# Decode-token mixing and slot assignment moved into the tile loop of the output projection

## Chip, cores and metric

The kernel runs on 1 core of one Trainium2 chip. The metric is the device time of one execution in microseconds (us).

## What is computed

One inference step of a one-layer decoder, all in float32, for a prompt of 2048 tokens and for 8 decode samples of one token each ("the sample"). Cut to what matters here:

```python
h  = rmsnorm(x, norm_mix_g); z = h @ w_in                  # 1024 -> 3584 columns
hg = hgrn2_recurrence(...)                                 # 4 heads, state 128 x 128
att = merge_dilations(three windows (128,1), (512,4), (2048,16))   # 8 heads of 64
x  = x + concat(rmsnorm(hg) * silu(zg), att) @ w_out       # 1024 -> 1024
h2 = rmsnorm(x, norm_ffn_g)
group, experts, gates = hier_route(h2, w_rg, w_re)         # 1 of 8 groups, 2 of its 8 experts
x  = x + sum_k gates[k] * (silu(h2 @ w_g[e_k]) * (h2 @ w_u[e_k])) @ w_d[e_k]   # 64 experts, 512 wide
y  = rmsnorm(x, norm_final_g)
```

For the sample the recurrence is one step on a stored state (8 x 4 heads of 128 x 128), and attention reads 3 x 128 rows for each sample out of key and value caches.

## The kernel before

The program is a row of stages. Each is a block of its own: its tensors and semaphores are made at its start, and between stages all engines meet at a barrier. All waits are written out by hand (`wait_ge` on a semaphore, `then_inc` on the instruction that is waited for), and each engine works through its own list in order. SP issues DMAs on one queue, ACT and POOL on queues of their own.

1. `project_and_hgrn`: input projection and recurrence, 17 tiles of 128 tokens (16 of the prompt, one that holds the 8 samples). What the samples need is left in HBM in `S["sample"]`.
2. `prompt_attention`: 48 units of banded attention in 72 groups. SP loads queries, keys and 24 value tiles `v1`, then for each unit stores its result rows `att_rows` and loads further value tiles. VectorE (DVE) can't start the fifth unit's scores before the first unit's rows are stored (`ROWS_HELD = 4`).
3. `sample_mixer`: the same for the samples. SP loads the rows, four broadcasts to 128 partitions (`aq_wide`, `ak_wide`, `wide`), the state and six 2 MB windows of the caches. POOL updates the state (three operations on 128 x 4096), DVE multiplies keys and queries and reduces them (L1191, L1193), TensorE (PE) reads the state (L1117) and weighs the values (L1137), and the result goes to HBM as `catT_sample`.
4. `project_out_and_route`, "the out stage": 17 tiles. For each tile PE runs 16 matmuls of 512 columns against `w_out` (L1414, each recorded as two), turns the next tile's attention rows (L1400), turns the normalised rows `h2` of the tile before (L1385) and multiplies them with the routing weights (L1391). DVE does, in this order: merge the three attention patterns of the next tile (L1533 to L1554), add the input to each half of the product (L1573), copy the turned attention (L1560), scale the turned `h2` (L1525, "the drains"), the mean and the refinement of 1/sqrt with a wait for ACT between them (L105 to L111), and the routing of the tile before (L1483 to L1515). PE can't begin the routing matmuls before the drains are done, nor the next tile's product before the routing matmuls.
5. `assign_slots`: with all tiles routed it counts tokens for each expert, ranks them by matmuls, gives each (token, choice) a slot, scatters the token numbers to the slots in HBM by 34 indirect DMAs of POOL, one after the other (L1657), and reads the table back (L1645). Experts 0 and 1's weights are loaded meanwhile.
6. `experts`: 64 blocks of up to 96 rows, one for each expert, with weights of 6 MB each in two buffers: gate and up (L1897, L1906), down (L1925, L1929).
7. `combine`: gathers each token's two rows, adds, normalises, stores.

Of the kernel before, what the change touches and what calls it, by code (L numbers as in the profile page):

```python
# [7 lines left out]
F32 = mybir.dt.float32  # L8
# [8 lines left out]
P = 128  # L17
# [745 lines left out]
def prompt_attention(nc, A, S):  # L763
# [16 lines left out]
    with ExitStack() as ctx:  # L780
# [3 lines left out]
        qT = sb("aqT", [P, PAIRS, SEQ])  # L784
        kT = sb("akT", [P, PAIRS, SEQ])
# [11 lines left out]
        consts_in, ones_ready = sem("consts_in2"), sem("ones_ready2")  # L797
# [13 lines left out]
        def _(sp):  # L811
# [28 lines left out]
            for x in range(TILES, V_SLOTS):  # L840
                load_v(x)
            for k in range(NU):
                store(k)
                for x in range(NU - V_SLOTS):
                    if k == (x + 1 if x < TILES else x + DILATIONS[1]):
                        load_v(x + V_SLOTS)
            for b in range(ROWS_HELD):
                sp.wait_ge(rows_stored[b], 16 * (NU // ROWS_HELD))

# [150 lines left out]

def sample_constants():
    heads = np.zeros((NS, ATW), np.float32)
    for h in range(ATH):
        heads[h, h * ATD:(h + 1) * ATD] = 1.0
    to_row = np.zeros((NS, NS, NS), np.float32)
    for b in range(NS):
        to_row[:, b, b] = 1.0
# [4 lines left out]


def sample_mixer(nc, A, S):


    with ExitStack() as ctx:
        sb = lambda n, s, d=F32: ctx.enter_context(nc.sbuf_tensor(n, s, d))
        ps = lambda n, s: ctx.enter_context(nc.psum_tensor(n, s, F32))
        sem = semaphores(nc, ctx)  # L1020
        NH = NS * ATH
        rows = sb("s_rows", [NS, 8, 512])
        ident = sb("ident3", [P, P])
        own_head = sb("own_head", [NS, ATW])
        to_row = sb("to_row", [NS, NS, NS])
        head_gain = sb("head_gain3", [P, HGH])
        state = sb("s_state", [P, NS, HGH, HGD])
        wide = sb("wide", [P, NS, HGW])
        aq_wide = sb("aq_wide", [P, NS, ATW])
        ak_wide = sb("ak_wide", [P, NS, ATW])  # L1030
        av_row = sb("av_row", [1, NS, ATW])
        keys = sb("s_keys", [P, 2, NS, ATW])
        values = sb("s_values", [P, 3, NS, ATW])
        cols = sb("s_cols", [P, 3, HGH, NS])
        q_diag = sb("q_diag", [P, HGH, NS * NS])
        scores = sb("s_scores", [P, 4, NH])
        peak = sb("s_peak", [NH, 1])
        probs = sb("s_probs", [NH, 4 * P])
        den = sb("s_den", [NH, 1])
        probsT = sb("s_probsT", [P, 4, NH])  # L1040
        picked = sb("s_picked", [NS, 2, ATW])
        cat = sb("s_cat", [NS, D])
        catT = sb("s_catT", [P, KT, NS])
        junk = sb("s_junk", [NS, HGD])
        o_sum, o_mean, o_guess, o_tmp, o_rstd = (sb(n, [NS, HGH]) for n in ("so_sum", "so_mean", "so_guess", "so_tmp", "so_rstd"))
        cols_ps = ps("cols_ps", [P, 3, HGH, NS])
        o_ps = ps("so_ps", [NS, HGW])
        sT_ps = ps("sT_ps", [NH, 4 * P])
        pT_ps = ps("pT_ps", [P, 4, NH])
        pv_ps = [ps(f"pv_ps{i}", [NS, ATW]) for i in range(2)]  # L1050
        att_ps = ps("att_ps", [NS, ATW])
        catT_ps = ps("catT_ps", [P, KT, NS])

        aq_in, ak_in = sem("aq_in3"), sem("ak_in3")
        rows_in, state_in, wide_in, values_in, stored = (sem(n) for n in ("rows_in", "state_in", "wide_in", "values_in", "stored3"))
        keys_in = [sem(f"keys_in{p}") for p in range(3)]
# [1135 lines left out]
```

## Time and profile before

| | |
|---|---|
| median of 3 runs (lowest, highest) | 3520.1 us (3516.5, 3521.5) |
| profiled execution: its own time, its span | 3525.5 us, 3523.7 us |
| PE busy, share of span | 3000.1 us, 85% |
| DVE | 2035.7 us, 58% |
| ACT | 927.1 us, 26% |
| POOL | 340.7 us, 10% |
| mean granted TensorE clock | 0.924 |

The span is the time from the first to the last instruction of the profiled execution. Busy shares are means over stages that have different limits. The granted clock is 1.0 at 2.4 GHz and 0.5 at 1.2 GHz. An idle time before an instruction is shown with what ended it.

### The profile page before, as it was taken

Reading aid. Unit: us, or ns where it says so; the run is one execution under the profiler, and the core shown is the slowest. Engines: PE = TensorE matmul, PEld = TensorE weight load, DVE = VectorE, ACT = ScalarE, POOL = GpSimd, SP = SyncE. Lnnn points to the kernel's source line nnn. Section 1 sums busy time; section 2 is a strip of 40 time slices with the busy share of each in tenths; the row PEclk is TensorE's granted clock in tenths of the full one; section 3 lists DMA queues with packets and bytes.
Section 4 is the critical chain, followed back from the end, with each engine's and each line's share of the span. In section 5 each row is a group of like instructions: output and inputs, shape, how many; then the busy total and the mean of one; then the engine's idle time right before and its main releaser. Section 6 shows DMA issues by size and latency. Waiting matters only on the chain. (4 is left out here: it accounts for less than half of the span.)

```text
span 3523.7 us, 48806 instructions
## 1 busy us (share of the span) xinstructions
PE 3000.1 (85%) x17843; PEld 1569.0 (45%) x17843; DVE 2035.7 (58%) x3851; ACT 927.1 (26%) x1786; POOL 340.7 (10%) x314
## 2 busy tenths in 40 slices
PE   8999999999999967998159996399999999999920
PEld 3555544555545546877014443144444444444400
DVE  4666666666666644555425665266666666666645
ACT  2222222222322224544003332022222222222223
POOL 0111111111111100000300000400000000000023
PEclk9999999999999978999579997699999999999965
DMA  8122112221112144532933433399999999999956
GB/s 297 48 100 75 68 68 73 104 96 70 68 68 79 64 127 117 157 107 92 255 98 121 148 131 136 110 409 412 414 415 416 411 411 408 414 412 411 392 196 228
DMA packets 205640, 724.75 MB, mean 206 GB/s; under 512 B 68456, under 2 KB 107112, under 8 KB 179960
## 3 DMA queue, kind: packets, MB, share of 16 engines
q1 hardware_dynamic: 178240, 638.92, 48.1%
q0 software_dynamic: 17280, 59.34, 4.8%
q10 hardware_dynamic: 10048, 25.57, 2.0%
q8 instruction: 40, 0.66, 0.1%
q14 instruction: 32, 0.26, 0.0%
HBM read 619.32 MB, written 171.57 MB: 224 GB/s over the span
## 5 line engine op out<-in xcount | busy, mean ns | idle before, releaser
L361 PE MATMUL z_ps<-w_in,xT 128*128 128x512 f32 x1904 | 862.2, 607 | 6.0 <-DMA w_in<-in_w_in_dram 6.0
L361 PEld LDWEIGHTS z_ps<-w_in,xT 128*128 128x128 f32 x1904 | 363.1, 196 | 425.1 <-issue 420.7
L1897 PE MATMUL a_ps<-w_gate,xT 128*64 128x512 f32 x1024 | 455.8, 598 | 3.4 <-DVE hidden L1985 2.8
L1897 PE MATMUL a_ps<-w_up,xT 128*64 128x512 f32 x1024 | 455.8, 598 | 0.0
L1897 PEld LDWEIGHTS a_ps<-w_gate,xT 128*64 128x64 f32 x1024 | 135.6, 137 | 287.2 <-issue 286.2
L1969 DVE COPY hiddenT<-h_ps 128x384 f32<-128x384 f32 x64 | 35.7, 557 | 387.6 <-PE h_ps L1915 387.6
L1414 PE MATMUL o_ps<-w_out,catT 128*128 128x512 f32 x544 | 248.6, 617 | 1.9 <-issue 1.0
L530 POOL TENSOR_TENSOR kd<-decay,kT 128x896 f32<-128x896 f32 x64 | 133.0, 2078 | 1093.5 <-ACT decay L446 1093.5
L1925 PE MATMUL ya_ps<-w_down,hiddenT 128*64 128x512 f32 x1024 | 235.5, 602 | 1.3 <-ACT y L1854 1.3
L615 DVE TENSOR_TENSOR masked<-p_ps,pair_masks 128x1024 f32<-128x1024 f32 x64 | 78.4, 1224 | 271.0 <-PE p_ps L325 271.0
L1906 PE MATMUL b_ps<-w_up,xT 128*32 128x256 f32 x2048 | 233.4, 380 | 0.0
L1906 PE MATMUL b_ps<-w_gate,xT 128*32 128x256 f32 x2048 | 233.4, 380 | 0.0
L1981 DVE RECIPROCAL sig_a<-sig_a 64x512 f32<-64x512 f32 x64 | 214.1, 3345 | 2.2
L975 DVE CUSTOM_DVE_ANT_0 probs<-s_ps,masks 128x256 f32<-128x256 f32 (+1 forms) x384 | 115.8, 362 | 154.1 <-PE s_ps L882 104.8
L943 ACT ACTIVATE probs<-probs,att_rows 128x256 f32<-128x256 f32 (+1 forms) x384 | 143.5, 449 | 184.4 <-DVE att_rows L975 184.3
L918 PE MATMUL ao_ps<-v,probsT 128*128 128x65 f32 x1200 | 154.8, 284 | 23.0 <-DVE probsT L984 23.0
L596 DVE RECIPROCAL sig<-sig 128x512 f32<-128x512 f32 x51 | 171.0, 3353 | 1.8
L918 PEld LDWEIGHTS ao_ps<-v,probsT 128*128 128x128 f32 x1200 | 144.4, 197 | 54.9 <-issue 33.3
L1414 PEld LDWEIGHTS o_ps<-w_out,catT 128*128 128x128 f32 x544 | 106.2, 198 | 131.8 <-issue 131.8
L1851 ACT ACTIVATE y<-ya_ps 64x512 f32<-64x512 f32 x128 | 75.8, 592 | 328.9 <-PE yb_ps L1929 327.4
L604 DVE TENSOR_TENSOR qd<-decay,qT 128x896 f32<-128x896 f32 x64 | 159.9, 2499 | 0.0
L1906 PEld LDWEIGHTS b_ps<-w_gate,xT 128*32 128x32 f32 x2048 | 113.7, 110 | 84.3
(304 smaller groups left out, 4245.9 us busy)
## 6 DMA issues: line engine op xcount, KB each, us to landing
w_gate<-in_w_expert_gate_dram SPq DMA_DIRECT2D x64, 2048.0 KB, 11.1
w_up<-in_w_expert_up_dram SPq DMA_DIRECT2D x64, 2048.0 KB, 18.4
w_down<-in_w_expert_down_dram SPq DMA_DIRECT2D x64, 2048.0 KB, 26.3
scratch_y_slots<-y ACTq DMA_DIRECT2D x64, 384.0 KB, 10.4
scratch_y_slots<-blank POOLq DMA_DIRECT2D x6, 2688.0 KB, 14.8
w_in<-in_w_in_dram SPq DMA_DIRECT2D x7, 2048.0 KB, 17.9
scratch_att<-att_rows SPq DMA_DIRECT2D x48, 264.0 KB, 2.2
parts<-scratch_att SPq DMA_DIRECT2D x16, 792.0 KB, 6.5
```

The costliest lines, as they stand in the source:

```text
L361: last = nc.tensor.matmul(z_ps[(u + g) % 2][:], xT[:, u, t, :], w_in[:, t, Z_COLUMN[g]:Z_COLUMN[g] + 512], start=(t == 0), stop=(t == KT - 1))
L530: nc.gpsimd.tensor_tensor(kd[:], decay[:, 0:LEVELS, :], bcast(kT[:, h:h + 1, :], (P, LEVELS, P)), ALU.mult).then_inc(kd_ready, 1)
L596: nc.vector.reciprocal(sig[:], sig[:]).then_inc(steps, 1)
L604: nc.vector.tensor_tensor(qd[:], decay[:, 0:LEVELS, :], bcast(qT[:, h:h + 1, :], (P, LEVELS, P)), ALU.mult).then_inc(qd_ready, 1)
L918: last = nc.tensor.matmul(out, probsT[:, g % 2, a, at:at + P], v1[:, x % V_SLOTS, h, :], start=(j == 0), stop=(j == len(tiles) - 1))
L943: last = nc.scalar.activation(probs[:, g % 2, a, at], probs[:, g % 2, a, at], ACT.Exp, scale=-1.0, bias=rows[:, k % ROWS_HELD, h, ROW - 1: ...
L975: last = nc.vector.tensor_tensor_reduce(probs[:, g % 2, a, at], s_ps[g % 2][a][:, at], masks[:, 2 * P - n:], 1.0, FAR, ALU.add, ALU.min, r ...
L1414: last = nc.tensor.matmul(o_ps[half][:], cT[:, c, :], w_out[:, c, half * 512:half * 512 + 512], start=(c == 0), stop=(c == KT - 1))
L1897: last = nc.tensor.matmul(a_ps[k * WIDE:(k + 1) * WIDE, :], xT[:, u, c, 0:WIDE], w[:, u, c, :], start=(c == 0), stop=(c == KT - 1))
L1906: last = nc.tensor.matmul(b_ps[k * REST:(k + 1) * REST, :], xT[:, u, c, WIDE:CAP], w[:, u, c, k % 2 * Q:k % 2 * Q + Q], start=(c == 0), st ...
L1925: nc.tensor.matmul(ya_ps[k * WIDE:(k + 1) * WIDE, :], hiddenT[:, c, 0:WIDE], w_down[:, u, c, k * 512:k * 512 + 512], start=(c == 0), stop= ...
L1981: nc.vector.reciprocal(sig_a[:], sig_a[:]).then_inc(sig_a_steps, 1)
```

## The change

- `sample_mixer` is gone. Its work stands in pieces in the out stage: POOL issues its loads on its own queue (queries, state, value broadcast, windows of the caches) and now also does the three products of keys and queries; `sample_piece(n)` on DVE, `if n == ...` on PE and ACT do the rest in the tiles named. Its big tensors lie in the buffers of the experts' gate and up weights, `W`. The new token's own key is multiplied on 64 partitions instead of broadcast, and the values of four samples are weighed side by side in four column groups of PE.
- `assign_slots` is gone. Each tile is ranked two tiles later: two small matmuls `rank` on PE, `place` and `add_table` on DVE, and `fill_table`, a product of one-hot matrices that writes the token numbers by (expert, rank) into a table. What is left, counts and the expert of each block, follows the last tile. The slots of tokens ranked beyond 96 are worked out in `experts` (`finish_slots`), whose POOL puts one indirect store behind each of the first 34 row gathers.
- The out stage is written out for all tiles instead of looped. Its weights and constants are loaded by SP in `prompt_attention`, between the last first-round value tile and the first store. Experts 0 and 1's gate and up weights are loaded in tiles 13 and 14 (4 MB each), down weights 0 and 1 at the start of `experts`.

```diff
@@ prompt_attention @@
             for x in range(TILES, V_SLOTS):
                 load_v(x)
+            load_out_weights(sp, A, O, out_loaded)
             for k in range(NU):
                 store(k)
...
+def load_out_weights(eng, A, O, arrived):
+    for half in range(2):
+        t = slice(half * KT // 2, (half + 1) * KT // 2)
+        eng.dma_start(O["w_out"][:, t, :], A["w_out"][0].rearrange("(t p) n -> p t n", p=P)[:, t, :]).then_inc(arrived, 16)
+    eng.dma_start(O["w_route"][:, 0], A["w_route_group"][0].rearrange("(p t) g -> p t g", p=P)).then_inc(arrived, 16)
+    for g in range(GROUPS):
+        eng.dma_start(O["w_route"][:, g + 1], A["w_route_expert"][0, g].rearrange("(p t) e -> p t e", p=P)).then_inc(arrived, 16)
+    load_ffn_gain(eng, O["ffn_gain"], A, arrived)
+    for name in ("iota", "real_row", "before"):
+        eng.dma_start(O[name][:], A[name]).then_inc(arrived, 16)
...
@@ project_out_and_route, SP @@
+            load_parts(0)
+            sp.dma_start(ident[:], A["ident"]).then_inc(consts_in, 16)
+            load(0)
+            load_parts(1)
+            for dst, src in ((own_head, A["own_head"]), (to_row, A["to_row"]), (head_gain, A["head_gain"]),
+                             (row_number, A["row_number"])):
+                sp.dma_start(dst[:], src).then_inc(consts_in, 16)
+            load(1)
...
+                if n == 13:
+                    sp.wait_ge(pv_done, 2)
+                    sp.wait_ge(state_stored, 16)
+                    load_expert(sp, A, "w_expert_gate", W["gate"][:, 0], 0, weights_in)
+                    load_expert(sp, A, "w_expert_up", W["up"][:, 0], 0, weights_in)
...
@@ POOL @@
+            nc.gpsimd.tensor_tensor(state, state, per_column(2), ALU.mult).then_inc(state_steps, 1)
+            pool.wait_ge(wide_in, 16)
+            nc.gpsimd.tensor_tensor(v, v, per_column(1), ALU.mult).then_inc(state_steps, 1)
+            pool.wait_ge(state_steps, 2)
+            nc.gpsimd.tensor_tensor(state, state, v, ALU.add).then_inc(state_done, 1)
...
+            for p in range(3):
+                pool.wait_ge(keys_in[p], 16)
+                nc.gpsimd.tensor_tensor(ring[p % 2], ring[p % 2], aq_wide, ALU.mult).then_inc(products, 1)
...
@@ PE @@
+            def project(n, half):
+                u = n % 2
+                if half == 0:
+                    if n < TILES:
+                        pe.wait_ge(cat_in[u], 16 * (n // 2) + 16)
+                        pe.wait_ge(attT_ready, n + 1)
+                    else:
+                        pe.wait_ge(catT_ready, 2)
...
+            pe.wait_ge(consts_in, 16 * 5)
+            turn_att(0)
+            for n in range(NT + 2):
+                if n < NT:
+                    project(n, 0)
+                if n >= 2:
+                    rank(n - 2)
+                if n < NT:
+                    project(n, 1)
+                if n >= 2:
+                    fill_table(n - 2)
+                if n + 1 < TILES:
+                    turn_att(n + 1)
+                if 1 <= n <= NT:
+                    post(n - 1)
...
+                if n == 3:
+                    pe.wait_ge(diag_ready, 2)
+                    pe.wait_ge(state_done, 1)
+                    for h in range(HGH):
+                        for b in range(NS):
+                            last = nc.tensor.matmul(s_ps[1][0:NS, h * HGD:(h + 1) * HGD], q_diag[:, h, b * NS:(b + 1) * NS],
+                                                    state[:, b, h, :], start=(b == 0), stop=(b == NS - 1))
+                    last.then_inc(o_filled, 1)
...
+                if n in (10, 12):
+                    if n == 10:
+                        pe.wait_ge(probsT_ready, 3)
+                    for p in ((0, 1) if n == 10 else (2, 3)):
+                        pe.wait_ge(values_in[p] if p < 3 else av_in, 16)
+                        for r in range(2):
+                            for i in range(4):
+                                b = 4 * r + i
+                                out = s_ps[r][GROUP * i:GROUP * (i + 1), :]
+                                if p < 3:
+                                    last = nc.tensor.matmul(out, probsT[:, p, b, :], ring[1 - p % 2][:, b, :], start=(p == 0), stop=False,
+                                                            tile_position=(0, GROUP * i))
+                                else:
+                                    last = nc.tensor.matmul(out, probsT[0:1, 3, b, :], av_row[:, b, :], start=False, stop=True,
+                                                            tile_position=(0, GROUP * i))
+                    last.then_inc(pv_done, 1)
...
@@ DVE @@
+            def place(m):
+                dve.wait_ge(ranked, m + 1)
+                nc.vector.tensor_tensor(own_rank[:], R["chosen"][:, m], rank_ps.unsqueeze(1).broadcast_to([P, 2, EXPERTS]), ALU.mult)\
+                  .then_inc(rank_steps, 1)
+                dve.wait_ge(rank_steps, m + 1)
+                if m:
+                    dve.wait_ge(tabled, m)
+                nc.vector.reduce_sum(R["rank"][:, m, :], own_rank[:], axis=AX.X).then_inc(ranks_set, 1)
+                nc.vector.tensor_scalar(numbers[:, :, 0, :], R["chosen"][:, m], row_number[:, 0:1], None, ALU.mult)
+                nc.vector.tensor_scalar(numbers[:, :, 1, :], R["chosen"][:, m], float(m), None, ALU.mult)
+                dve.wait_ge(ranks_set, m + 1)
+                for k in range(2):
+                    last = nc.vector.tensor_scalar(at_rank[:, k, :], iota[:, 0:CAP], R["rank"][:, m, k:k + 1], None, ALU.is_equal)
+                last.then_inc(numbers_ready, 1)
+
+            def add_table(m):
+                dve.wait_ge(tabled, m + 1)
+                if m:
+                    dve.wait_ge(table_added, m)
+                nc.vector.tensor_tensor(table[:], table[:], table_ps, ALU.add).then_inc(table_added, 1)
...
+                if n in (3, 4, 6):
+                    p = (3, 4, 6).index(n)
+                    dve.wait_ge(products, p + 1)
+                    nc.vector.reduce_sum(scores[:, p, :], ring[p % 2].rearrange("p b (h e) -> p (b h) e", e=ATD), axis=AX.X)\
+                      .then_inc(score_ready, 1)
...
+                if n == 15:
+                    dve.wait_ge(catT_filled, 1)
+                    dve.wait_ge(o_done, 2 * TILES - 2)
...
+            for n in range(NT + 2):
+                if n + 1 < TILES:
+                    merge(n + 1)
+                if n < NT:
+                    add_input(n, 0)
+                if n >= 2:
+                    place(n - 2)
+                if n < NT:
+                    add_input(n, 1)
+                if n >= 2:
+                    add_table(n - 2)
+                if n + 1 < TILES:
+                    put_att(n + 1)
+                if 1 <= n <= NT:
+                    drains(n - 1)
...
+                if 1 <= n <= NT:
+                    routing(n - 1)
+                sample_piece(n)
...
@@ experts, POOL @@
+            for b in range(SCATTERS):
+                gather(b + 2, b % 2, 2)
...
+                scatter_late(b // 2, b % 2)
```

PE, out stage, one tile and the start of the next. `h` is `h2`. Before, in every tile:

```order
L1414 MATMUL o_ps<-w_out,catT 128x512 x16
L1400 MATMUL a_ps<-ident,att 128x128 x4
L1385 MATMUL t_ps<-ident,h 128x128 x8
L1391 MATMUL l_ps<-w_route,h2T 128x72 x8
L1414 MATMUL o_ps<-w_out,catT 128x512 x16
```

Now, at the turn from the tile with n = 3 to that with n = 4 (`s_ps`, `w_up` and `q_diag` are the samples' output, their states and their queries):

```order
L1319 MATMUL t_ps<-ident,h 128x128 x8
L1326 MATMUL l_ps<-w_route,h2T 128x72 x8
L1368 MATMUL s_ps<-w_up,q_diag 8x128 x32
L1307 MATMUL o_ps<-w_out,catT 128x512 x8
L1331 MATMUL l_ps<-taken,before_bf 128x64
L1332 MATMUL l_ps<-so_far,ones_bf 128x64
L1307 MATMUL o_ps<-w_out,catT 128x512 x8
L1337 MATMUL l_ps<-at_rank,numbers 128x96 x2
L1293 MATMUL a_ps<-ident,att 128x128 x4
```

The product's two halves stand apart, with the ranking between them and the table behind them, and 32 matmuls of the state stand ahead of the product of tile 4.

DVE, out stage, one tile from the end of the merge of attention patterns to the mean. Before:

```order
L1548 TENSOR_TENSOR scaled<-parts,part_den 128x1536
L1554 TENSOR_REDUCE att<-scaled 128x512
L1573 TENSOR_TENSOR xr<-o_ps,xr 128x512 x2
L1560 COPY catT<-a_ps 128x512
L1525 TENSOR_TENSOR h2T<-t_ps,ffn_gain 128x512 x2
L1579 TENSOR_SCALAR mean<-ssq 128x1
```

The same stretch now:

```order
L1569 TENSOR_TENSOR scaled<-parts,part_den 128x1536
L1575 TENSOR_REDUCE att<-scaled 128x512
L1588 TENSOR_TENSOR xr<-o_ps,xr 128x512
L1522 TENSOR_TENSOR own_rank<-chosen,l_ps 128x128
L1527 TENSOR_REDUCE rank<-own_rank 128x2
L1528 TENSOR_SCALAR numbers<-chosen,row_number 128x2x64
L1529 TENSOR_SCALAR numbers<-chosen 128x2x64
L1532 TENSOR_SCALAR at_rank<-iota,rank 128x96 x2
L1588 TENSOR_TENSOR xr<-o_ps,xr 128x512
L1539 TENSOR_TENSOR table<-table,l_ps 128x96
L1581 COPY catT<-a_ps 128x512
L1545 TENSOR_TENSOR h2T<-t_ps,ffn_gain 128x512 x2
```

`place` has come between the two additions of the input, and `add_table` between the second and the drains.

SP, `prompt_attention`, the end of the first round of loads. Before, the store of the first unit's rows follows the value tiles at once:

```order
L816 DMA v<-out_new_v_prompt_dram 128x8x64 x12
L828 DMA scratch_att<-att_rows 128x528 x2
```

Now 22 loads stand in between:

```order
L815 DMA v<-out_new_v_prompt_dram 128x8x64 x12
L1043 DMA w_out<-in_w_out_dram 128x4x1024 x2
L1044 DMA w_route<-in_w_route_group_dram 128x64
L1046 DMA w_route<-in_w_route_expert_dram 128x64 x8
L1033 DMA ffn_gain<-in_ffn_gain_dram 16x8x1 x8
L1049 DMA iota<-in_iota_dram 128x128
L1049 DMA real_row<-in_real_row_dram 128x1
L1049 DMA before<-in_before_dram 128x128
L827 DMA scratch_att<-att_rows 128x528 x2
```

## Rows read from the trace of the kernel before

**Rows 1.** Busy time by stage: us, each engine, granted clock, DMA share, GB/s.

```profile
1665.80:1813.10 147.30, 51.79 (x172) 15.65 (x172) 47.53 (x36) 4.99 (x13) 27.05 (x3) 0.65 0.58 159
1813.10:1844.10 31.00, 1.08 (x4) 0.74 (x5) 7.61 (x14) 0.22 (x1) 0.00 (x0) 0.50 0.71 232
1844.10:2175.20 331.10, 304.45 (x1012) 161.38 (x1012) 195.13 (x735) 115.82 (x182) 0.00 (x0) 0.95 0.36 124
2181.10:2250.50 69.40, 3.28 (x39) 2.37 (x39) 20.39 (x58) 0.00 (x0) 32.94 (x35) 0.50 0.39 155
2300.00:3340.00 1040.00, 1040.00 (x9454) 436.56 (x9452) 648.09 (x785) 219.69 (x482) 65.23 (x120) 1.00 1.01 412
```

**Rows 2.** Timeline, sample stage and start of the out stage: start, us, engine, line.

```profile
1665.77 0.30 SPq L1081 DMA_DIRECT2D s_rows<-scratch_sample  x1
...
1813.08 0.38 SPq L1336 DMA_DIRECT2D w_out<-in_w_out_dram  x1
...
1836.48 0.17 DVE L1533 TENSOR_TENSOR least<-parts 128x8 f32<-128x8 f32 x1 [21.11 <-DMA w_route<-in_w_route_expert_dram]
...
1844.11 17.00 PE L1414 MATMUL o_ps<-w_out,catT 128*128 128x512 f32 x32 [0.88 <-DVE catT L1560]
```

**Rows 3.** Timeline, one tile of the out stage.

```profile
2032.92 13.95 PE L1414 MATMUL o_ps<-w_out,catT 128*128 128x512 f32 x32
...
2046.90 0.69 DVE L1573 TENSOR_TENSOR xr<-o_ps,xr 128x512 f32<-128x512 f32 x1 [1.57 <-PE o_ps L1414]
...
2049.44 2.00 PE L1391 MATMUL l_ps<-w_route,h2T 128*128 128x72 f32 x16 [1.27 <-DVE h2T L1525]
...
2051.28 15.64 PE L1414 MATMUL o_ps<-w_out,catT 128*128 128x512 f32 x32
...
2051.84 0.16 DVE L105 TENSOR_TENSOR tmp<-guess 128x1 f32<-128x1 f32 x1 [2.39 <-ACT guess L100]
```

**Rows 4.** Timeline, slot assignment and the first DMA of the experts.

```profile
2188.61 0.24 PE L1671 MATMUL count_ps<-so_far,ones_bf 128*128 128x64 bf16 x1
2191.97 0.59 PE L1673 MATMUL expert_ps<-ident,expert_of 128*1 128x128 f32 x2 [3.12 <-DVE expert_of L1711]
...
2250.50 0.33 SPq L1795 DMA_DIRECT2D ident<-in_ident_dram  x1
```

**Rows 5.** Timeline, POOL and DVE at work together (two places).

```profile
621.92 2.08 POOL L530 TENSOR_TENSOR kd<-decay,kT 128x896 f32<-128x896 f32 x1 [9.32 <-ACT decay L446]
622.20 2.74 DVE L604 TENSOR_TENSOR qd<-decay,qT 128x896 f32<-128x896 f32 x1
...
1717.18 7.09 POOL L1171 TENSOR_TENSOR s_state<-s_state,s_cols 128x4096 f32<-128x4096 f32 x1 [125.29 <-DMA s_state<-in_state_hgrn_dram]
...
1736.09 4.79 DVE L1191 TENSOR_TENSOR s_keys<-s_keys,aq_wide 128x4096 f32<-128x4096 f32 x1 [16.44 <-DMA s_keys<-in_cache_attn_k_dram]
1736.67 12.88 POOL L1176 TENSOR_TENSOR s_state<-s_state,wide 128x4096 f32<-128x4096 f32 x1
```

**Rows 6.** Timeline, attention stage: SP's value loads, DVE's wait for a store.

```profile
1321.28 16.67 SPq L816 DMA_DIRECT2D v<-out_new_v_prompt_dram  x12
...
1342.14 0.42 DVE L975 CUSTOM_DVE_ANT_0 probs<-s_ps,masks 128x256 f32<-128x256 f32 x1 [22.18 <-DMA scratch_att<-att_rows]
```

**Rows 7.** DMA issues by line: size, us to landing.

```profile
parts<-scratch_att SPq DMA_DIRECT2D x16, 792.0 KB, 6.5
...
w_out<-in_w_out_dram SPq DMA_DIRECT2D x1, 4096.0 KB, 15.1
```

**Rows 8.** Groups: busy us, mean ns of one, idle before.

```profile
L608 DVE TENSOR_TENSOR q_start<-decay,qT 128x128 f32<-128x128 f32 x64 | 17.8, 279 | 0.0
...
L1193 DVE TENSOR_REDUCE s_scores<-s_keys 128x64 f32<-128x4096 f32 x3 | 13.3, 4419 | 0.1
```

**Rows 9.** Timeline, PE in the attention stage before and after a wait.

```profile
1600.61 2.00 PE L918 MATMUL ao_ps<-v,probsT 128*128 128x65 f32 x16
...
1607.76 3.55 PE L918 MATMUL ao_ps<-v,probsT 128*128 128x65 f32 x16 [2.24 <-DVE probsT L984]
```

More of the change, by code:

```diff
@@ new lines, in project_out_and_route @@
+        own_rank = sb("own_rank", [P, 2, EXPERTS])
+        at_rank = sb("at_rank", [P, 2, CAP], BF16)
+        numbers = sb("numbers", [P, 2, 2, EXPERTS], BF16)
+        table = sb("table", [P, CAP])
+        count, count_i = sb("count", [P, EXPERTS]), sb("count_i", [P, EXPERTS], I32)
+        blocks, through, ones, passed = (sb(n, [P, EXPERTS]) for n in ("blocks", "through", "ones5", "passed"))
+        expert_of = sb("expert_of", [P, 1])
+        zero_table = sb("zero_table", [MORE_BLOCKS + 2, CAP], I32)
@@ L1324, in project_out_and_route @@
         route = sem("route_steps4")
-        ROUTE_STEPS = 20
-        block = ctx.enter_context(nc.Block())
-        def more(n, ahead):
-            return not (isinstance(n, int) and n + ahead >= TILES)
-        def buffers(n, u):
-            return (catT[2], xr[2]) if isinstance(n, int) and n == TILES else (catT[u], xr[u])
+        taken_ready, ranked, rank_steps, numbers_ready, tabled, table_added = (
+            sem(n + "4") for n in ("taken_ready", "ranked", "rank_steps", "numbers_ready", "tabled", "table_added"))
@@ L1372, in _ @@
+            store(LAST)
+            sp.wait_ge(zeroed, 16)
+            sp.wait_ge(weights_in, 64)
             for u in range(2):
@@ L1422, in _, with rank, fill_table @@
-            out_turns(pe, body)
-            post(TILES, 0, 1)
+            def rank(m):
+                pe.wait_ge(taken_ready, 2 * m + 3)
+                nc.tensor.matmul(rank_ps, before_bf[:], taken[:], start=True, stop=False)
+                nc.tensor.matmul(rank_ps, ones_bf[:], so_far[:, m % 2, :], start=False, stop=True).then_inc(ranked, 1)
+            def fill_table(m):
+                pe.wait_ge(numbers_ready, m + 1)
+                for k in range(2):
+                    last = nc.tensor.matmul(table_ps, numbers[:, k].rearrange("p a e -> p (a e)"), at_rank[:, k, :],
+                                            start=(k == 0), stop=(k == 1))
+                last.then_inc(tabled, 1)
@@ L1587, in _ @@
-            out_turns(dve, body)
-            drains(TILES)
-            routing(TILES, 1)
-            for k in range(2):
-                dve.wait_ge(route, ROUTE_STEPS * NT)
-                nc.vector.tensor_scalar(R["chosen"][k][:, TILES, :], R["chosen"][k][:, TILES, :], real_row[:], None, ALU.mult)\
-                  .then_inc(route, 1)
-            dve.wait_ge(route, ROUTE_STEPS * NT + 2)
-def load_expert(eng, A, name, dst, expert, arrived):
-    eng.dma_start(dst, A[name][0, bass.ds(expert, 1), :, :].rearrange("o (p t) n -> p (o t) n", p=P)).then_inc(arrived, 16)
@@ L1698, in _ @@
             dve.wait_ge(counted, 1)
-            chain(nc.vector.tensor_scalar(count[:], count_ps[:], -1.0, 0.0, ALU.add, ALU.max))
+            chain(nc.vector.tensor_scalar(count[:], count_ps, -1.0, 0.0, ALU.add, ALU.max))
             chain(nc.vector.tensor_copy(count_i[:], count[:]))
@@ L1811, in _ @@
             n = pairs(sp)
+            down(0, 0, 0)
+            down(1, 1, 0)
             gate_up(2, 0)
-            down(1, 1, 1)
             gate_up(3, 1)
```

901 lines of the change are left out of this document (419 added, 482 removed).

## The prediction

> **What bounds the kernel now.** I read the busy time by stage first. From 2300 us on the experts keep TensorE (PE) busy for 1040.0 of 1040.0 us at granted clock 1.00, with the DMA engines full too (share 1.01, 412 GB/s) [rows 1]: the change can't shorten that stage, only what stands ahead of it. There are three such pieces. The sample stage takes 147.3 us with PE busy for 51.8 and DVE for 47.5 of them [rows 1], from its first load to the first load of the out stage [rows 2]. The out stage needs 31.0 us before its first product, of which DVE waits 21.11 for routing weights [rows 1, 2]. The slot assignment holds PE for 3.3 and POOL for 32.9 of its 69.4 us [rows 1]. The out stage itself is a loop bound by PE: 304.5 of 331.1 us busy [rows 1], and its tile is 18.36 us (from 2032.92 to 2051.28), of which 13.95 is the product [rows 3]. So whatever is moved into it costs nothing only if it fits into DVE's pauses, and costs its full length if it is PE work. DVE's pauses in a tile are 1.57 us ahead of the addition and 2.39 us ahead of the refinement [rows 3]; DVE is busy 195.1 of 331.1 us [rows 1].
>
> **What is removed.** The sample stage, -147.3. The out stage's start goes from 31.0 to about 21: its weights are there already, but PE waits for five constants, the last of which stand on SP's queue behind some 2.6 MB of tile loads. At the 232 GB/s of the same stretch [rows 1] that is 11.3 us alone and 22.6 if POOL's queue, which starts its state and its broadcasts at the same moment, takes half; I take 19, near the upper one, and 2 for turning and copying: -10 (between -17 and -6). The assignment goes from 69.4 to what must follow the last tile, counts and the expert of each block: from the count matmul to the next one, 12 DVE operations, 3.36 us [rows 4], so 0.28 each, and about 25 such operations stay: 7. With two barriers' worth of ends 7.5: -61.9. Together -219.2.
>
> **What is added.**
>
> Attention: 22 loads of 4.5 MB go ahead of the first store. DVE already stands 22.18 us there, because that store waits behind the value loads on SP's queue [rows 6], so nothing hides them. 4.5 MB at 412 GB/s [rows 1] are 10.9 us, and the 18 small ones are given 1.6: +12.5. It is no less than 0 if DVE were to find other work (there is none in the order), and about 15.1, what the 4 MB load took before from issue to landing [rows 7], is the upper bound.
>
> Each of 15 tiles: the two rank matmuls of 64 columns and the two of 96 are bf16 and short (0.24 for one of 64 columns [rows 4]), 0.2 beyond what the pipeline hides, and `add_table` (0.25) stands ahead of the drains, for which PE waits [rows 3]: 0.45 x 15 = +7. `place` has six operations; an operation on 128x128 is 0.279 [rows 8], so 1.6 us in all, and it fits just into DVE's 1.57 us pause between merge and the second addition [rows 3]. I cost it at nothing, and the cover is then used up: PE and DVE are level in every tile with it.
>
> The sample's pieces on PE, at the product's rate (8192 columns in 13.95 us [rows 3]): 32 state matmuls of 128 columns at n = 3 are 7.0; 16 matmuls of 512 columns at n = 10 and at n = 12, 13.95 each if one after the other and 3.5 if four run side by side, which they are written for: 3.6 each; two of 512 columns at n = 13, 1.8. On DVE: the reduction of 128x4096 is 4.42 [rows 8], at n = 3 beside PE's 7.0 and so free, at n = 4 and n = 6 on the path because the next merge and drains come behind it (4.4 and, with the small chain of that tile, 6.5); the chains at n = 8 1.9 and elsewhere 3. Sum +32. At n = 15 the last tile's product waits for `catT_ready`, which DVE sets only behind the routing of tile 14 and after both halves of product 15: about a third of a tile, +6.
>
> POOL beside DVE. A DVE product of two SBUF inputs that begins while POOL computes ends 0.94 us after POOL does (624.94 against 624.00) [rows 5], and all 64 such pairs read alike; and POOL's third state operation took 12.88, of which DVE's product, begun ahead of it, still ran for 4.21 (1740.88 - 1736.67): 8.67 by itself, the first one 7.09 [rows 5]. So the two lock each other out for a whole operation. In the out stage the merges are such DVE operations (the multiplication with shares, the maxima). Three state operations, 7.1 + 7.1 + 8.7 = 22.9 us nearly at once, start in the merge of tile 1 and hold DVE up; its pauses of that tile, 1.57 + 2.39, hide 4.0 of it: +19. Three products of 8.7 us, hit at a random place, hold DVE for 5 each, and a pause or so of each hides 4 in all: +11. With both +30 (between 0, if each falls on additions from PSUM and reductions, and 48, the whole 49.0 us). The Trainium skill, page SBUF — State Buffer, section Who interferes with whom, says the same of two-input operations, adds that `tensor_scalar` and copies can take the shared port pair too while a reduction never does, and by that `place` would be held too, about 3 us more; it is not in the sum.
>
> Clock: after a wait of 2.24 us PE's 16 matmuls took 3.55 in place of 2.00 [rows 9], and a product took 15.64 in place of 13.95 after a tile turn [rows 3]. Every stall named above is such a wait, some eight of them at 1.5: +12 (0 to 25). The weights of experts 0 and 1 stand on SP's queue ahead of the loads of tiles 14 and 15, 8.4 MB or 20 us at 412 GB/s, against an 18.4 us tile and two tiles' lead: +3. Ends of `place` and `add_table` behind the last tile +2.
>
> In `experts` 34 indirect stores (32.9 us of POOL before [rows 1]) and `finish_slots` (25 operations, 7 us of DVE) lie beside PE's 1040 us, in which POOL is busy for 65.2: 0.
>
> Added: 12.5 + 7 + 32 + 6 + 30 + 12 + 3 + 2 = 104.5. Net -114.7. The profiled execution took 3525.5, 5.4 above the median of 3520.1; the sum is made against it (3410.8), and against the median it gives **3405**.
>
> **Is the data there in time?** The samples' queries are turned at the end of tile 0, about 38 us into the stage. State by 62, first product by 71; its reduction stands at the end of tile 3, at 95 or later. The second window of keys is asked for at 62 and multiplied by 92, needed at 120; the third is asked for behind the first reduction and has two tiles. No piece should wait for its data.
>
> **Rivals.**
>
> (a) As worked, 3405: chance 0.55.
>
> (b) The lock costs next to nothing, because DVE's work in most of the tile reads PSUM or one input, and POOL's products fall there: 30 down to 5, and two of the clock's waits less, 3405 - 25 - 5 = 3375. For it: additions and drains read PSUM. Against it: the merge is about a third of DVE's tile. Chance 0.20.
>
> (c) DVE becomes the bound of every tile. `place` reads two `chosen` planes and waits twice for its own results; if its six operations and their waits come to 3.6 instead of 1.6, each of 15 tiles is 2 us longer, +30: 3435. It decides from 1.6 on, so there is no margin. Chance 0.13.
>
> (d) POOL's queue, some 21 MB (ten of 2 MB) in the first 12 tiles, slows the tile's loads: `parts` landed 6.5 us after issue [rows 7] and the next merge needs it within a tile. At 21 MB in 220 us, 95 GB/s beside the present 124 [rows 1], the average fits, but the two broadcasts to all partitions fill the engines at a lower rate; with 8 us in each of three tiles, +23: 3428. The same page and section of the Trainium skill holds that DMAs from the POOL queue are starved while DVE runs a two-port copy, because their descriptors are made by POOL; no row here shows it, and it would make this case later, not the tiles. Chance 0.09.
>
> (e) Slower than before. The many short stalls keep PE at 1.2 GHz in the out stage, as it is in the sample stage and the assignment (granted clock 0.65 and 0.50 [rows 1]), in place of 0.95. A tile's 17.9 us of PE work (304.5 over 17 tiles) would take 17.5 more; from 115 / 17.5 = 6.6 such tiles on the gain is gone, and with all 17 it is +297: 3700. Against it: the clock stays at 0.95 in the present loop with its pauses of 1.3 us. Chance 0.03.
>
> **How the numbers follow.** All uncertain terms at their low ends (attention 0, lock 0, clock 0, start 14) give 3345; (c) with the lock at 48 gives 3453. That holds (a) to (d) with small misses: 3345 to 3455. Faster by over 0.2% (7 us, about what a measurement of this kernel tells from no change) in all of (a) to (d): 0.96; within it 0.01; slower 0.03.
>
> **What would show it.** In the changed profile: the attention stage with DVE's one wait at about 35 us in place of 22.18; the first product of the out stage about 21 us behind its first load; a plain tile (n = 8 or 11) of 18.8 us with the product at 13.95; PE's largest waits in tiles 1 and 2, ended by DVE while POOL computes, and merge operations that end with a POOL operation; from the last routing to the first expert's load some 8 us; the experts unchanged. The prediction is wrong if plain tiles are over 20 us (then (c)), if merges stretch without POOL or wait for `parts` (then (d)), if POOL's operations show no DVE operation ending with them (then (b)), or if the granted clock of the stage is under 0.85 (then (e)).

## The result and the profile after

The changed kernel takes 3573.1 us (median of 4 runs, 3563.5 to 3584.3) against 3518.3 us before: a ratio of 1.0157, with a 95% interval of 1.0126 to 1.0188. It is slower, by 1.6%, and the forecast was 3405. Its profiled execution has a span of 3582.1 us, 58.4 more than the one before.

The page first: granted clock, busy share of the DMA engines and GB/s in 40 slices of the span, some 90 us each.

```profile
span 3582.1 us, 48236 instructions
...
PEclk9999999999999978998798979999998999999965
DMA  7121113211122073544544519999999999999956
GB/s 293 64 87 68 67 69 108 92 67 67 67 103 92 16 202 95 154 130 124 184 166 142 210 59 285 318 321 314 318 314 312 322 350 412 411 412 408 411 207 226
```

The experts fill the slices from the 25th on. From the 34th to the 38th they look as they did before, 408 to 412 GB/s. But in the seven from the 26th to the 32nd the DMA engines are just as busy (9) and move only 312 to 322 GB/s. By stage (us, each engine's busy time, granted clock, DMA share, GB/s):

```profile
1696.50:2112.00 415.50, 344.78 (x1211) 181.69 (x1211) 270.12 (x835) 118.06 (x191) 56.35 (x13) 0.87 0.48 160
2112.00:2139.09 27.09, 7.77 (x36) 5.84 (x36) 16.66 (x92) 3.79 (x9) 0.00 (x1) 0.52 0.10 40
2139.09:2931.00 791.91, 663.11 (x5492) 280.88 (x5496) 385.44 (x484) 125.51 (x275) 78.18 (x113) 0.92 1.00 312
2931.00:3260.00 329.00, 328.33 (x2996) 139.89 (x2990) 204.82 (x248) 69.26 (x152) 20.66 (x38) 1.00 1.01 411
```

The last two rows are one stage. Before, it had PE busy throughout and 412 GB/s at a share of 1.01 [rows 1]. Now, over the first 792 us of it, PE is busy for 663.1 and the share is 1.00 at 312 GB/s; behind 2931 us it is 411 again. What PE waits for there (us in total, times, longest; `issue` is idle time for which the profile shows no wait):

```profile
PE a_ps L1910 <- issue: 60.2, 17, 5.4
PE a_ps L1910 <- DMA w_up<-in_w_expert_up_dram: 56.5, 16, 6.0
```

Four marks give the ledger of the whole: the out stage's first load, its first product, the last ranking, the experts' first load.

```profile
1676.80 0.38 SPq L1191 DMA_DIRECT2D parts<-scratch_att  x1
...
1704.38 16.87 PE L1307 MATMUL o_ps<-w_out,catT 128*128 128x512 f32 x32 [0.87 <-DVE catT L1581]
...
2129.61 0.24 PE L1331 MATMUL l_ps<-taken,before_bf 128*128 128x64 bf16 x1 [3.79 <-DVE taken L1507]
...
2139.09 0.34 SPq L1788 DMA_DIRECT2D ident<-in_ident_dram  x1
```

Ahead of the experts the change does what it should: their first load stands at 2139.09 in place of 2250.50 [rows 4], 111.4 us earlier, where my terms give 114.7. Five of the kernels below have the same out stage, and in their profiles the experts begin at 2123.11 to 2138.74, so this profile is at the late end of that spread. From there to the end it takes 1443.0 us in place of 1273.2: +169.8. The two make the 58.4. So the whole surprise lies behind the experts' first load, in the stage that I had priced at nothing.

In it each of the first 34 blocks has one new thing, an indirect store. One block of them: POOL's issue of the store, and the stretches before its words are written, while they are, and after.

```profile
2407.15 1.02 POOL L1836 DMA_INDIRECT scratch_late_token<-token,late  x1 [0.30 <-issue]
...
2407.00:2416.00 9.00, 9.00 (x40) 3.20 (x37) 0.02 (x1) 0.65 (x2) 1.02 (x1) 0.84 1.00 396
2417.00:2424.00 7.00, 7.00 (x84) 2.94 (x80) 6.83 (x8) 0.38 (x1) 0.00 (x0) 1.00 1.08 173
2425.00:2430.00 5.00, 1.61 (x18) 0.64 (x12) 1.84 (x5) 2.68 (x6) 2.11 (x3) 1.00 1.00 426
```

The 128 words stand in the trace as 16 packets of 32 B, 8 words in each. They come behind the row gather's, from 2415.93 to 2417.20, and take under 20 ns each; the first weight packet of over 1.2 us begins at 2417.05. For the next 7 us the DMA engines are busy (1.08) and move 173 GB/s, not 396 or 426. The packets of the weights (16 KB each), counted from the trace over 600 us of this stage, show the same:

```
before (2400:3000)   13427 packets, mean 635 ns, median 615, over 1200 ns:  0.0%
after  (2300:2900)   10263 packets, mean 857 ns, median 611, over 1200 ns:  9.7%
```

Most packets are as fast as ever, and one in ten takes twice as long or more, up to 6.4 us. What differs from the 34 stores of the old assignment is where the words go. There each word had a slot of its own, and no full stream of weights ran beside them (DMA share 0.39 [rows 1]). Here nearly all tokens have no late slot, and partition r then writes to word `SPARE + r`: 128 words in 512 adjacent bytes. Theory A is that these stores hold up the weights' packets, and A1 that they do so because their words share a small piece of memory and get in each other's way. Rivals within it are A2, any store of this size does it, and A3, it is the same addresses again and again. Rival B is something else in the stage.

### The profile page after: what moved, and what is told of

Read it like the earlier page. It is cut to its first block and busy times, and to the rows that moved or that the text cites. A ratio compares the mean times of both kernels' runs of the same rounds, so it can differ in the third digit from the quotient of the medians.

```text
span 3582.1 us, 48236 instructions
## 1 busy us (share of the span) xinstructions
PE 3038.3 (85%) x17863; PEld 1601.0 (45%) x17863; DVE 2061.4 (58%) x3938; ACT 927.5 (26%) x1787; POOL 382.7 (11%) x337
## 5 line engine op out<-in xcount | busy, mean ns | idle before, releaser
L1910 PE MATMUL a_ps<-w_gate,xT 128*64 128x512 f32 x1024 | 505.4, 651 | 121.5 <-issue 60.2
L1910 PE MATMUL a_ps<-w_up,xT 128*64 128x512 f32 x1024 | 506.4, 652 | 0.0
L1910 PEld LDWEIGHTS a_ps<-w_gate,xT 128*64 128x64 f32 x1024 | 147.3, 149 | 429.9 <-issue 428.9
L1307 PE MATMUL o_ps<-w_out,catT 128*128 128x512 f32 x544 | 256.5, 630 | 7.5 <-DVE catT L1653 6.4
L1876 ACT ACTIVATE exp_a<-a_ps 64x512 f32<-64x512 f32 x64 | 37.8, 591 | 468.4 <-PE a_ps L1910 468.4
```

The source lines that it names most:

```text
L1307: last = nc.tensor.matmul(o_ps[half][:], catT[u][:, c, :], w_out[:, c, half * 512:half * 512 + 512], start=(c == 0), stop=(c == KT - 1))
L1910: last = nc.tensor.matmul(a_ps[k * WIDE:(k + 1) * WIDE, :], xT[:, u, c, 0:WIDE], w[:, u, c, :], start=(c == 0), stop=(c == KT - 1))
```

## The experiments

"Before" ran on the same chip with each batch (medians 3514.5 to 3518.4). Ratios are against it.

**1. No stores.** In `experts` the loop keeps its gathers and loses the stores; what is left out is the late table, so tokens ranked beyond 96 get no row of their own.

```diff
-                if b == 0:
-                    pool.wait_ge(late_ready, 1)
-                else:
-                    pool.wait_ge(scattered, 16 * b)
-                scatter_late(b // 2, b % 2)
-            pool.wait_ge(scattered, 16 * SCATTERS)
```

> The changed kernel without the 34 indirect stores of the experts stage (left out: the tokens ranked beyond 96 of their expert get no slot in the late table). Theory A (the stores slow the weights' packets, whatever else was moved): the experts stage is back at about 17.2 us a block from the first block on, DMA at 411 GB/s, and the kernel takes 3573 - 165 = about 3405 us. Rival B (something else of the change slows the first half of the experts: the order of the weight buffers, the small DVE work, the row gathers): about 3570 us, and the blocks stay at 22 us.

Measured: 3407.3 us, ratio 0.9684 (0.9668 to 0.9700). B falls: the stores are the whole loss. (The profiled one of its five executions took 6341 us, with PE busy for 6039 of them, and isn't read; I have no account of it. The other four agree within 9 us.)

**2 and 3. Addresses 64 B and 512 B apart.**

```diff
                 chain(nc.vector.tensor_copy(own_row[:], token[:, 0:1]))
+                chain(nc.vector.tensor_scalar(own_row[:], own_row[:], 16.0, None, ALU.mult))
```

(128.0 for 512 B; the scratch table is made longer by as much.)

> The same 34 stores, but the words of tokens that have no late slot go to addresses 64 B apart in place of 4 B apart. Theory A1 (128 writes into the same 512 B get in each other's way, about 60 ns each): about 3410 us if 64 B apart is far enough; A2 (any store of 128 words of 4 B costs the weights 7 us, wherever it goes): no change, 3573 us; A3 (it is the same addresses written again and again): no change, 3573 us.

> As before with 512 B between the addresses. A1 with a wider neighbourhood than 64 B: about 3410 us here while 64 B is still near 3573, or between. A2 and A3: 3573 us.

Measured: 3406.1 (0.9678, 0.9662 to 0.9695) and 3407.2 (0.9689, 0.9673 to 0.9705). Both equal the kernel without stores. The same number of words of the same size, written to the same addresses in all 34 stores, costs nothing once they are 64 B apart, so A2 and A3 fall. The experts' first 792 us in the 64 B kernel:

```profile
2139.09:2931.00 791.91, 786.03 (x7094) 334.40 (x7096) 497.41 (x609) 162.64 (x356) 87.02 (x127) 1.00 1.00 403
```

PE is busy for 786.0 in place of 663.1 us, at 403 GB/s in place of 312.

**4. The kernel before with these stores alone.**

```diff
...
+            for b in range(34):
+                gather(b + 2, b % 2, 2)
+                if b:
+                    pool.wait_ge(dumped, 16 * b)
+                pool.indirect_dma_start(out=S["dump"], out_offset=bass.IndirectOffsetOnAxis(ap=own_row[:], axis=0),
+                                        in_=own_row[:], in_offset=None).then_inc(dumped, 16)
...
```

> The kernel before with one part of the change alone: 34 indirect stores of 128 words to 512 adjacent bytes, one behind each of the first 34 row gathers of the experts stage (they go to a scratch tensor of their own and change nothing of the result). Theory A: 3518 + 34 x 4.9 = about 3685 us, blocks of 22 us while they last. Rival B: 3518 us, no change.

Measured: 3678.7 us, 1.0460 (1.0442 to 1.0477), 160 above before and 4.7 us for each store. While they last, and after:

```profile
2300.00:3000.00 700.00, 574.69 (x4880) 245.67 (x4874) 334.22 (x408) 115.91 (x254) 66.67 (x95) 0.93 1.00 317
3060.00:3400.00 340.00, 339.94 (x3082) 142.78 (x3072) 212.50 (x256) 72.47 (x159) 21.98 (x40) 1.00 1.01 413
```

The cost needs nothing else of the change.

**5 and 6. How near is too near.** The factor of experiment 2 is 2.0 for 8 B and 8.0 for 32 B.

> The changed kernel with 8 B between the addresses of the stores (4 B apart it takes 3573, 64 B apart 3406). If the cost is by words that share 64 B (16 at 4 B apart, 8 at 8 B, 1 at 64 B) and each word but the first costs the same, 3406 + 167 x 7/8 = about 3550 if 8 words in 64 B wait as 16 do, word by word; if it goes by the number of pairs it is about 3480. If only words directly side by side hurt, 3406.

> The changed kernel with 32 B between the addresses (4 B: 3573, 8 B: 3481, 64 B: 3406). The cost was 167 for 16 words in 64 B and 75 for 8, about 11 for each word beyond the first: if 64 B is what counts, 2 words in it give 3417; if the piece is 32 B or smaller, 3406.

Measured: at 8 B 3481.0 (0.9895, 0.9878 to 0.9913), at 32 B 3404.6 (0.9684, 0.9669 to 0.9699). So 32 B apart is free: with two words in each 64 B there is no sign of the 11 us that a cost by the word would give. The numbers fit pieces of 32 B, where 8 words in one cost 167 and 4 cost 75 (7 words beyond the first by 23.9 give 167, and 3 of them 72), but they don't show them. A spacing of 16 B was not tried, and in all these kernels the stretch that the 128 words cover grows with their spacing: 512 B, 1 KB, 4 KB, 8 KB and 64 KB. A cost by the words in a larger piece, or by the length of the stretch, fits the same times. Full groups of 8 adjacent words, the groups far apart, would tell them from each other; that was not run. The Trainium skill, page Collectives: The Full Stack, section Rules for kernel authors, asks for the buffers of collectives to be aligned to 32 bytes, since the hardware otherwise reads, modifies and writes. Whether that happens here no run shows: a lone word of 4 B in each 32 B fills none of them either, and costs nothing. What costs is many separate writes close together.

**7. The same 512 bytes in another order.**

```diff
+                chain(nc.vector.tensor_scalar(in_eight[:], token[:, 0:1], 7, 4, ALU.bitwise_and, ALU.logical_shift_left))
+                chain(nc.vector.tensor_scalar(eighth[:], token[:, 0:1], 3, None, ALU.logical_shift_right))
+                chain(nc.vector.tensor_tensor(in_eight[:], in_eight[:], eighth[:], ALU.bitwise_or))
+                chain(nc.vector.tensor_copy(own_row[:], in_eight[:]))
```

> The changed kernel with the same 512 B of addresses, but partition r writes word 16 (r mod 8) + r / 8: words side by side in memory come from partitions 8 apart, and neighbouring partitions write 64 B apart. If what costs is that one 64 B piece gets 16 separate writes, whoever makes them: 3573 us. If it is writes that follow each other directly in the list of one DMA engine: much less, down to 3406.

Measured: 3554.0 (1.0122, 1.0097 to 1.0146), 148 of the 167 us. That writes are neighbours in the list explains at most the other 19, which is about the spread of the changed kernel's own runs (3563.5 to 3584.3).

```profile
2350.00:2850.00 500.00, 424.63 (x3582) 181.49 (x3580) 245.83 (x299) 84.03 (x184) 48.61 (x69) 0.93 1.01 323
```

**8. Constants waited for later.** The remaining experiments take up terms of my sum, all on the 64 B kernel (3406.1).

```diff
-            pe.wait_ge(consts_in, 16 * 5)
+            pe.wait_ge(ident_in, 16)
```

(PE waits for the rest at n = 13, DVE at n = 2.)

> With the stores 64 B apart (3406 us): PE and DVE wait for the four constants of the later pieces only where they need them, not ahead of the first tile. Theory: the wait of 29.3 us for row_number at the start of the out stage is the constants' place behind the second tile's parts; the first product starts about 12 us earlier, 3394 us. Rival: the first tile's own rows come as late, since POOL's loads take half of the DMA: 0 to -3 us.

Measured: 3406.8 (0.9693, 0.9678 to 0.9708), no gain: the rival's number, by another way. The three rows are from PE's, DVE's and again PE's timeline.

```profile
1694.41 6.02 PE L1307 MATMUL o_ps<-w_out,catT 128*128 128x512 f32 x10 [0.87 <-DVE catT L1582]
...
1728.16 1.93 DVE L1555 TENSOR_TENSOR least<-parts 128x8 f32<-128x8 f32 x1 [12.11 <-DMA parts<-scratch_att]
...
1754.62 1.12 PE L1293 MATMUL a_ps<-ident,att 128*128 128x128 f32 x4 [25.56 <-DVE att L1576]
```

The first product starts at 1694.41, 12.97 us behind the stage's first load at 1681.44; in the 64 B kernel it is 23.26 (1681.04 to 1704.30). But then the merge of tile 2 waits 12.11 us for its parts, and behind that for POOL, and PE waits 25.56 in place of 18.18 for it.

**9. Weights loaded behind the 31st store.**

```diff
-            load_out_weights(sp, A, O, out_loaded)
             for k in range(NU):
                 store(k)
+                if k == 30:
+                    load_out_weights(sp, A, O, out_loaded)
```

> With the stores 64 B apart (3406 us): the 22 loads of the out stage's weights and constants are issued behind the 31st store of the attention stage, in place of ahead of the first. Theory (my term of +12.5): DVE's one long wait there is back at about 22 us and the kernel takes 11 us less, 3395 us. Rival: the loads now delay stores or value loads later on: no gain.

Measured: 3395.7 (0.9653, 0.9637 to 0.9668), 10.4 less, as the theory has it. The intervals of the two ratios overlap a little (0.9662 to 0.9668), but the profiles bear it out: from its first load to the next stage's, the attention stage takes 401.2 to 405.5 us in the eight kernels with the loads ahead of the stores, and 388.7 to 393.9 in the three with the loads behind. DVE's long wait there, which is 30.89 in the 64 B kernel, is only 5.0 shorter here and not back at 22, so the mark that I had given for it is met in part:

```profile
1340.16 0.42 DVE L977 CUSTOM_DVE_ANT_0 probs<-s_ps,masks 128x256 f32<-128x256 f32 x1 [25.87 <-DMA scratch_att<-att_rows]
```

**10. State operations on DVE.**

```diff
-            nc.gpsimd.tensor_tensor(state, state, per_column(2), ALU.mult).then_inc(state_steps, 1)
...
+                    dve.wait_ge(state_in, 16)
+                    nc.vector.tensor_tensor(state, state, per_column(2), ALU.mult).then_inc(state_steps, 1)
```

> With the stores 64 B apart (3406 us): the three state operations run on DVE, behind tile 0, and no longer on POOL. Theory (the lock: three DVE operations of the merge each end with one of POOL's, 22.6 us in all): DVE needs 3 x 4.8 = 14.4 us for them, so the stall is 8 us shorter, 3398 us. Rival (DVE's long operations in the merge wait for something else than POOL's): the merge stays as long and the 14.4 us come on top, about 3420 us.

Measured: 3403.1 (0.9679, 0.9666 to 0.9692), not told apart from 3406.1. The timeline shows why neither number came:

```profile
1743.21 10.30 DVE L1557 TENSOR_TENSOR part_den<-share_of,whole_den 128x24 f32<-128x24 f32 x1
...
1744.65 8.82 POOL L1265 TENSOR_TENSOR w_gate<-w_gate,w_up 128x4096 f32<-128x4096 f32 x1
...
1765.20 8.82 POOL L1265 TENSOR_TENSOR w_gate<-w_gate,w_up 128x4096 f32<-128x4096 f32 x1 [11.73 <-DMA w_gate<-in_cache_attn_k_dram]
...
1765.71 8.33 DVE L1476 TENSOR_SCALAR in_group<-iota,group_at 128x8 f32<-128x8 f32 x1
```

The three state operations took 4.42 each, but the products that POOL then did earlier hit the same merge (10.30 us for an operation of 24 columns) and one of the routing, a `tensor_scalar` of 8 columns (8.33). The lock had moved, not gone.

**11 and 12. Products on DVE too, without and with the later constants.** Both also have experiment 9's loads.

> Stores 64 B apart, the out stage's weights loaded behind the 31st store, and both the state operations and the three products on DVE. With the state alone on DVE the lock moved on: POOL's products held a merge operation for 10.3 us and a tensor_scalar of the routing for 8.3. Theory (no POOL operation is left to lock): 3396 - 22.6 - 8.5 - 2 - 2 + 13.3 + 2 x 4.4 + 0.9 = about 3383 us. Rival (DVE's 4.4 us operations in tiles 3, 4 and 6 cost more than the lock's): 3396 us or more.

> The same with the constants waited for only where they are needed. With POOL's operations in place that started the first product 10 us earlier and gave all of it back in the merge of tile 2, which waited for its parts and then for POOL. Theory: with no POOL operation left, part of the 10 us stays, the rest is lost to the wait for the parts of tile 2: about 3378 us. Rival: all of it is lost to the parts, 3383 us.

Measured: 3384.9 (0.9625, 0.9612 to 0.9638) and 3390.1 (0.9635, 0.9618 to 0.9652). No POOL operation is left to lock, and the first is 10.8 below experiment 9's 3395.7, as expected, though here too the intervals just meet. With the constants nothing is gained on top. The first of them is the best version here, 130.7 us ahead of before in its batch (3515.6). Its experts begin at

```profile
2112.37 0.34 SPq L1788 DMA_DIRECT2D ident<-in_ident_dram  x1
```

and so 18.7 us earlier than in the 64 B kernel's profile (2131.05), and 10.7 earlier than in the earliest of those with the out stage unchanged (2123.11).

## Why the prediction was wrong

The step that failed is the line on `experts`: "34 indirect stores (32.9 us of POOL before [rows 1]) and `finish_slots` [...] lie beside PE's 1040 us, in which POOL is busy for 65.2: 0". I had priced the store's instruction on POOL and not its writes, in a stage whose DMA share was 1.01 [rows 1], that is, where a DMA engine's lost time is on the path. At a wider spacing of their addresses the same stores would have been free there, as experiments 2, 3 and 6 show. I had not asked where the words of the tokens go that are not late. The stores measured +169.8 in the profiled execution; by the runs, with and without them, 3573.1 - 3407.3 = 165.8 us. Without them the kernel takes 3407, against my 3405. That this is so near is partly luck: the terms below miss by up to 6.6 us one way and 3 the other, and the same out stage, from its first load to the experts', took between 441.8 and 462.3 us in six profiles. None of my five rivals was this one, and the one on the other side of the line (e) had the clock as its mechanism, which did not come about: 0.87 in the out stage, against 0.95 before.

The other steps, in the changed kernel's trace:

| term | predicted | measured |
|---|---|---|
| all ahead of the experts | -114.7 | -111.4 |
| attention stage | +12.5 | +14.5 (401.4 against 387.0, first load to the next stage's) |
| out stage, first load to first product | 21 | 27.6 (22.6 to 24.9 in the five kernels with the same out stage) |
| last ranking to the experts' first load | 9.5 | 9.5 |
| POOL's state operations, PE's wait | 19 | 18.2 |
| POOL's products, hold on DVE | 15 | 12.5 (operations of 1.96, 8.50, 2.60 less their own time) |
| state matmuls, n = 3 | 7.0 | 7.15 |
| values, n = 10 and 12 | 3.6 each | 5.24, 5.31 (at granted clock 0.68 and 0.71) |
| DVE's reductions at n = 4 and 6, PE's wait | 4.4, 6.5 | 5.43, 5.24 |
| experts' weights ahead of tile loads | 3 | no wait of PE for them |
| last product's wait | 6 | 6.4 |

**Attention.** Near in size, and experiment 9 shows most of it to be these loads. What I had named as its mark was off: DVE's one wait is 41.13, not 35, which is 19 longer than before, and the stage 14.5, so some 4 come back behind it.

```profile
1354.22 0.42 DVE L976 CUSTOM_DVE_ANT_0 probs<-s_ps,masks 128x256 f32<-128x256 f32 x1 [41.13 <-DMA scratch_att<-att_rows]
```

**Start of the out stage.** Mis-sized by 6.6 in this profile and by 1.6 to 3.9 in the five others: PE waits for the last constant, as I had said, but for longer. By experiment 8 it doesn't matter, since tile 2's parts are next.

```profile
PE a_ps L1293 <- DMA row_number<-in_row_number_dram: 29.3, 1, 29.3
...
PE a_ps L1293 <- DVE att L1575: 18.2, 1, 18.2
...
PE o_ps L1307 <- DVE catT L1653: 6.4, 1, 6.4
```

The third row is the last tile's product behind `catT_ready`.

**The lock.** Right in place and size. The three POOL operations hold one DVE operation of the merge each, of 8 or 24 columns:

```profile
1727.28 7.09 POOL L1262 TENSOR_TENSOR w_up<-w_up,s_cols 128x4096 f32<-128x4096 f32 x1 [41.27 <-DVE s_cols L1593]
1727.33 7.08 DVE L1554 TENSOR_TENSOR least<-parts 128x8 f32<-128x8 f32 x1
...
1734.35 7.08 POOL L1264 TENSOR_TENSOR w_gate<-w_gate,s_cols 128x4096 f32<-128x4096 f32 x1
...
1734.44 7.03 DVE L1556 TENSOR_TENSOR least<-least,parts 128x8 f32<-128x8 f32 x1
...
1741.51 8.86 POOL L1266 TENSOR_TENSOR w_up<-w_up,w_gate 128x4096 f32<-128x4096 f32 x1
...
1742.00 8.44 DVE L1560 TENSOR_TENSOR part_den<-share_of,parts 128x24 f32<-128x24 f32 x1 [0.29 <-ACT share_of L1421]
...
1754.90 1.12 PE L1293 MATMUL a_ps<-ident,att 128*128 128x128 f32 x4 [18.18 <-DVE att L1575]
...
1774.22 8.50 DVE L1528 TENSOR_SCALAR numbers<-chosen,row_number 128x128 bf16<-128x128 f32 x1
...
1783.27 0.34 PE L1337 MATMUL l_ps<-at_rank,numbers 128*128 128x96 bf16 x2 [8.83 <-DVE at_rank L1532]
```

The last but one is an operation of `place`, a `tensor_scalar` with one tensor (and its column of scalars) from SBUF, held 8.50 us by POOL's second product (1773.83 to 1782.63). Here the Trainium skill's rule (SBUF — State Buffer, Who interferes with whom), that a `tensor_scalar` can take the shared ports too, is seen in this kernel. I had left it out of the sum and put it at about 3 us. It is more: PE waits 8.83 us for this one operation, which is most of the 11 that the three products were given. DVE's next work was the addition from PSUM and the drains, and such operations ran at their own speed beside POOL.

**Plain tiles.** For n = 8 or 11 I had given 18.8 us. From one product's start to the next, n = 11 takes 19.0 (1978.35 to 1997.32) and n = 8 20.7 (1910.97 to 1931.68). Here is n = 9, its two halves and the next tile's start, and below them the granted clock (third from the end) early in the first half and in the second:

```profile
1931.68 8.78 PE L1307 MATMUL o_ps<-w_out,catT 128*128 128x512 f32 x16
...
1940.35 7.11 PE L1307 MATMUL o_ps<-w_out,catT 128*128 128x512 f32 x16
...
1952.59 8.80 PE L1307 MATMUL o_ps<-w_out,catT 128*128 128x512 f32 x16
...
1931.68:1935.00 3.32, 3.32 (x7) 1.46 (x7) 2.54 (x20) 2.50 (x4) 0.00 (x0) 0.56 0.00 0
1940.35:1947.30 6.95, 6.95 (x20) 3.03 (x19) 5.42 (x9) 0.00 (x0) 0.00 (x0) 1.00 0.41 147
```

It takes 20.9 us (0.6 of it the sample's transposes), and I had said that over 20 speaks for (c). It was not DVE, which itself waits 1.72 us for PE ahead of the second addition. The first half takes 8.78 in place of 7.11 at a granted clock of 0.56 over its first 3.3 us. From n = 9 on the clock falls so at the turn to every tile. Ahead of n = 11, 13 and 14 the fall meets the sample's matmuls (0.68, 0.71 and 0.60 over them), so that these products keep their 7.1 and the values take 5.2 and 5.3 instead. At the turns to n = 4, 5 and 7 it doesn't fall, with the same pause of 1.4 us for the drains; what decides it stays open. Before, five of 17 products took 15.6 in place of 13.95, so only part of this is the change's.

My clock term of 12 was for stalls, and there it is found: behind PE's waits for DVE ahead of the products of n = 2, 3, 6, 8 and 16 (18.18, 8.83, 5.43, 5.24 and 6.37 us) the work up to the end of the product's first half takes 0.7, 3.2, 4.5, 4.3 and 2.3 us longer than at full clock, an estimate from PE's timeline, 15 us in all. `place` fits, as costed, where no POOL operation holds it.

## What to carry to other kernels

That a store's instruction is hidden doesn't make the store free. Look where its words land: when most lanes have nothing to write and are sent to a dump, give each a dump address 32 B or more from the next. In a stage whose DMA share is at 1.0, price every new DMA by what it does to the bytes of others, and look at GB/s and not at the share, which stayed at 1.0 while the rate fell by a quarter. And long POOL operations are best placed where DVE works on inputs from PSUM or reduces; moved only in part, the lock moves along.

## What the runs showed of the hardware

- 128 words of 4 B written to 512 adjacent bytes held the weights' transfer for about 7 us (173 GB/s at a DMA share of 1.08) and cost 4.7 to 4.9 us of kernel time a store. 8 B apart it was 2.2 (75 us for 34), at 32, 64 or 512 B nothing that the runs can tell. Whether the measure is words in a piece of 32 B or the length of the stretch that they cover is not shown. That reads of other memory are held up with the writes is measured; where in the chip they meet stays open.
- A DVE operation of 8 or of 128 columns was held for 8.3 and 8.5 us by a POOL operation also where it was a `tensor_scalar`, with one tensor and a column of scalars from SBUF.
- Beside the same POOL operations (7.1 to 8.9 us), DVE's additions and copies of 512 columns with an input from PSUM took their usual 0.68 to 0.69 us, and a reduction of 128 columns 0.29.
